# One pool of 1-MB places for all expert weights, up products split by w1 and w3, and half of the shared expert and the ranking behind the first up products

## The reference, cut to what matters

```python
scores = sigmoid(xf @ w_router)             # 64 experts, 8 groups, 4 groups and 8 experts chosen per token
w = w / sum(w) * 2.5                        # the weights of the 8 chosen experts
def expert_block(args):
    toks, e, wts = args
    return swiglu(xpad[toks], w1[e], w3[e], w2[e]) * wts[:, None]
def swiglu(x, w1, w3, w2):
    return (silu(x @ w1) * (x @ w3)) @ w2   # w1, w3: 1024 x 256; w2: 256 x 1024
y = routed + swiglu(xf, ws1, ws3, ws2)      # the shared expert takes all tokens
```

## Time and profile before

| | |
|---|---|
| median of 3 runs | 2468.27 us |
| the profiled execution | 2467.98 us, span 2466.4 us |
| PE busy | 2324.8 us, 94% of the span |
| DVE, ACT, POOL busy | 34%, 23%, 5% |
| DMA moved | 672.94 MB, mean 273 GB/s |
| chain that ended last | PE 82%, DMA 9%, DVE 4% |

### The profile page before, as it was taken

One profiled execution on the slowest core, in us unless ns is written; L12 is line 12 of the kernel. 1 busy time (PEld: TensorE's weight loads), 2 busy tenths in 40 slices (PEclk: granted clock), 3 DMA queues, 4 the chain that ended last, 5 costly groups with the idle time before them and its releaser, 6 DMA issues.

```text
span 2466.4 us, 30431 instructions
## 1 busy us (share of the span) xinstructions
PE 2324.8 (94%) x11979; PEld 1543.9 (63%) x11979; DVE 845.8 (34%) x2149; ACT 568.6 (23%) x1227; POOL 122.6 (5%) x179
## 2 busy tenths in 40 slices
PE   7998999999999898998999989898998999999998
PEld 4857887555455454767896545554546787754764
DVE  0477633212212111297623212121211644421264
ACT  2233412111111112123302111111112433321254
POOL 4020000000000000010000000000000000001110
PEclk9999999999999998999999999999998999999999
DMA  9783583999999996953684999999986254240400
GB/s 334 264 311 118 206 328 132 418 415 414 413 404 414 417 400 248 319 197 137 225 326 183 407 414 414 417 395 414 415 368 190 92 186 143 84 145 29 159 1 18
DMA packets 206890, 672.94 MB, mean 273 GB/s; under 512 B 14000, under 2 KB 74648, under 8 KB 156816
## 3 DMA queue, kind: packets, MB, share of 16 engines
q1 hardware_dynamic: 200064, 656.87, 68.9%
q0 software_dynamic: 6240, 13.99, 1.7%
q10 hardware_dynamic: 432, 0.01, 0.0%
HBM read 661.38 MB, written 9.45 MB: 272 GB/s over the span
## 4 chain that ended last, share of the span: by engine, by line
PE 82%; DMA 9%; DVE 4%; ACT 2%; issue 2%; SPq 0%; ACTq 0%; POOL 0%; DVEq 0%
PE ps L278 46%; PE ps L2182 11%; PE ps L2217 7%; DMA ring<-in_ab_w_in 4%; PE ps L2233 3%; PE ps L1762 2%; DMA ring<-in_w 2%; DMA cst<-in_ab_w_in 2%; PE ps L1210 1%; DVE ar L1349 1%; PE ps L2864 1%; PE ps L3477 1%; PE ps L698 1%; DMA ring<-in_w_mod 1%; DMA ar<-in_w 1%
## 5 line engine op out<-in xcount | busy, mean ns | idle before, releaser
L278 PE MATMUL ps<-hT,ring 128*128 128x256 f32 (+2 forms) x2352 | 546.0, 388 | 3.4 <-ACT ar L1578 1.9
L278 PEld LDWEIGHTS ps<-hT,ring 128*128 128x128 f32 (+1 forms) x2352 | 442.2, 191 | 101.4 <-issue 37.1
L2182 PE MATMUL ps<-ring,ar 128*32 128x512 f32 (+2 forms) x1056 | 291.9, 613 | 20.2 <-DMA ring<-in_w 14.1
L2182 PE MATMUL ps<-ar 128*64 128x512 f32 (+1 forms) x992 | 292.3, 614 | 9.1 <-DMA ar<-in_w 9.0
L2182 PEld LDWEIGHTS ps<-ring,ar 128*32 128x32 f32 (+2 forms) x1056 | 90.7, 128 | 174.9 <-issue 162.0
L2217 PE MATMUL ps<-ring,ar 128*32 128x512 f32 (+2 forms) x808 | 182.3, 596 | 5.4 <-DVE ar L2365 3.0
L2499 DVE SCALAR_TENSOR_TENSOR exact_parts<-ps,ar,exact_parts 128x512 fp32r<-128x512 f32 x100 | 75.1, 751 | 284.5 <-ACT exact_parts L2345 278.9
L278 PE MATMUL ps<-xT,ring 128*128 128x256 f32 x576 | 134.6, 394 | 15.0 <-DMA ring<-in_ab_w_in 14.0
L2475 DVE TENSOR_TENSOR ar<-ar,ps 128x256 f32<-128x256 f32 x50 | 21.1, 421 | 351.3 <-ACT ar L2332 351.3
L278 PE MATMUL ps<-ring,ar 128*128 128x512 f32 x320 | 139.8, 593 | 0.9 <-DVE ar L3706 0.9
L2182 PEld LDWEIGHTS ps<-ar 128*64 128x64 f32 (+1 forms) x992 | 82.5, 126 | 91.4 <-issue 87.2
(11 more groups left out here) (461 smaller groups left out, 2782.2 us busy)
## 6 DMA issues: line engine op xcount, KB each, us to landing
ring<-in_w SPq DMA_DIRECT2D x233, 1024.0 KB, 15.9
ar<-in_w SPq DMA_DIRECT2D x124, 1024.0 KB, 12.8
ring<-in_w_mod SPq DMA_DIRECT2D x36, 2048.0 KB, 11.9
ring<-in_w_in SPq DMA_DIRECT2D x28, 2048.0 KB, 11.7
ring<-in_ab_w_in SPq DMA_DIRECT2D x51, 1024.0 KB, 10.9
cst<-in_w SPq DMA_DIRECT2D x27, 1024.0 KB, 12.5
ring<-in_w_out SPq DMA_DIRECT2D x4, 2048.0 KB, 10.5
ring<-in_ab_w_out SPq DMA_DIRECT2D x2, 4096.0 KB, 13.0
```

Of the source, the lines that this page charges most:

```text
L278: ins = te.matmul(o, l, r, start=(first and i == 0), stop=(last and i == len(pairs) - 1), skip_group_check=lax)
L2182: ins = te.matmul(b[cols, :], K.x_b[:, kk, in_pair(p, cols)], weights_up(K, l, r)[:, :, kk, :], start=(kk == 0), stop=(kk == 7))
```

## The change

Every expert matrix is now a load of its own (keys w1, w3, w2) with a place of its own. All 16 places form one pool: four halves of the wide buffers, the consts place, and the 11 places of the ring. The loads stand in the order in which the passes need them: w1 of all experts of a pass, then w3, then the fill, then w2. A place is given to the next load by when it comes free in that order. For the places of the ring the table `RING_HELD` says, for each layer, what the mixer left there. `pe_up` does the w1 products of the pass in one bank, with 256 columns each, and then the w3 products in another; w1's places are released in between. ACT takes silu behind the w1 products and DVE multiplies behind the w3 products. `pe_moe_start` leaves the second half of the shared expert's down products and the ranking to `pe_experts`, which does them between the first up products and the first turn. The transposed lists have another place in SBUF, since silu now writes their old one before the ranking reads them. Where the next stage begins in the ring is no longer the position behind the last load but a pair of places that comes free early (`next`).

```diff
+NOTHING, THIRD, OUT, ROUTER, SHARED_UP, SHARED_DOWN = -12, -10, -8, -6, -4, 0.5
+RING_HELD = [{1: NOTHING, 2: THIRD, 3: THIRD, 4: OUT, 5: OUT, 6: OUT, 7: OUT, 8: ROUTER, 9: SHARED_UP, 10: SHARED_UP,
+              0: SHARED_DOWN},
+             {10: NOTHING, 8: THIRD, 9: THIRD, 0: OUT, 1: OUT, 2: OUT, 3: OUT, 4: ROUTER, 5: SHARED_UP, 6: SHARED_UP,
+              7: SHARED_DOWN}]
+def in_turn(l):
+    out = []
+    for p, of in enumerate(PASS):
+        out += [(p, p + 0.3, "w1", r) for r, _ in of]
+        out += [(p + 0.3, p + 0.45, "w3", r) for r, _ in of]
+        if p in FILL_AT[l]:
+            out.append((p + 0.5, p + 0.65, "fill", FILL_AT[l][p]))
+        out += [(p + 0.7, p + 1, "w2", r) for r, _ in of]
+    return out
 def places(l):
-    up = {("wide", 0): (-1, None), ("wide", 1): (-1, None), **{("slot", n): (-1, None) for n in range(3)}}
-    down = {("consts", 0): (-1, None), ("last", 0): (-1, None), **{("half", u): (-1, None) for u in range(4)}}
+    free = {("consts", 0): (NOTHING, None), **{("wide", n): (THIRD, None) for n in range(4)},
+            **{("ring", u): (held, None) for u, held in RING_HELD[l].items()}}
...
+    for start, end, name, r in in_turn(l):
+        if l == 1 and start >= CONSTS_PASS:
+            free.pop(("consts", 0), None)
+        place = min(free, key=lambda k: free[k][0])
+        assert free[place][0] < start
+        out[name, r] = place, free[place][1]
+        free[place] = end, (name, r)
...
+    out["next"] = min(range(UNITS - 1), key=lambda u: max(free["ring", u][0], free["ring", u + 1][0]))
...
+            pos = K.where[key[1]]["next"]
...
 def pe_moe_start(K, l):
...
-    for n in range(4):
-        i, q = divmod(n, 2)
...
-        if n == 1:
-            yield from pe_first_slots(K, l)
-            yield from pe_selected(K, l, 0)
-            yield from pe_lists_turned(K, l)
-    yield from pe_lists_ranked(K, l)
+    yield from pe_shared_down(K, l, 0)
+    yield from pe_first_slots(K, l)
+    yield from pe_selected(K, l, 0)
+    yield from pe_lists_turned(K, l)
 def pe_up(K, l, p):
     te = K.te
...
+    for name, read in (("w1", "silu"), ("w3", "g")):
+        b = yield from K.bank((read, l, p))
...
+        for kk in range(8):
+            for r, cols in PASS[p]:
+                ins = te.matmul(b[cols, 0:256], K.x_b[:, kk, in_pair(p, cols)], w[r][:, kk, :], start=(kk == 0),
+                                stop=(kk == 7))
+        ins.then_inc(*K.pe(name, l, p, ps=b))
+        for r, _ in PASS[p]:
+            K.pe.also("used", name, l, r)
 def pe_experts(K, l):
...
         yield from pe_up(K, l, p)
+        if p == 0:
+            yield from pe_lists_ranked(K, l)
+            yield from pe_shared_down(K, l, 1)
 def act_experts(K, l):
...
-        ac.wait_ge(*(yield ("up", l, p)))
+        ac.wait_ge(*(yield ("w1", l, p)))
 def dve_experts(K, l):
...
         ve.wait_ge(*(yield ("silu", l, p)))
+        ve.wait_ge(*(yield ("w3", l, p)))
```

More of the change, by code:

```diff
@@ L419, in shared @@
         K.plan(("down", l, EXPERTS), 1, [(lambda f: k_major(f, D, 2), I["ws2"][l].rearrange("(j p) n -> p j n", j=2))])
[L421 to L443, removed]
     def experts(l):
@@ L451, in experts @@
         kind, r = K.where[0]["consts"]
[L452 to L457, removed]
+        consts = [("used", kind, 0, r)] if l else [("ctx_turned", 3)]
+        for _, _, name, r in in_turn(l):
+            (kind, u), last = where[name, r]
+            if name == "fill":
                 n, g = FILL[r]
                 src = abw.rearrange("(p k) n -> p k n", k=8)[:, :, FILL_COL[n] * D + g * 256:FILL_COL[n] * D + g * 256 + 256]
-                parts = [(lambda f: k_major(f, 256), src)]
+                part = (lambda f: k_major(f, 256)), src
             else:
-                parts = [(lambda f: f[:, 0:UNIT], ("w2", 2))]
-            if kind in ("slot", "half", "last"):
+                part = (lambda f: f[:, 0:UNIT]), (name, 2 if name == "w2" else 8)
+            if kind == "ring":
                 place = kind, u
             else:
-                start = first[kind][u] if kind == "wide" else first[kind]
-                place = views(name, kind, u), [("used", before[0], l, before[1])] if before else start
-            K.plan((name, l, r), len(parts), parts, place)
+                place = K.cst_place if kind == "consts" else K.wbuf[u // 2][:, u % 2, :]
+                place = place, [("used", last[0], l, last[1])] if last else wide[u // 2] if kind == "wide" else consts
+            K.plan((name, l, r), 1, [part], place)
     def ctx_parts(key, first, n):
@@ L572, in sp_program @@
     for n, (key, under, parts) in enumerate(K.loads):
-        if key[0] in ("up", "down") and FIXED <= key[2] < EXPERTS and key[1:] not in expert:
+        if key[0] in ("w1", "w3", "w2") and key[2] >= FIXED and key[1:] not in expert:
             sp.wait_ge(*(yield ("ranked", key[1])))
@@ L2209, in pe_down @@
     for r, _ in PASS[p]:
-        te.wait_ge(*(yield ("ring", "down", l, r)))
+        te.wait_ge(*(yield ("ring", "w2", l, r)))
     for q in range(2):
```

74 lines of the change are left out of this document (26 added, 48 removed).

## The result

| | median of runs | range | profiled execution |
|---|---|---|---|
| before, run again beside the changed kernel | 2465.91 us (16 runs) | 2463.28 to 2469.69 | 2467.98 us |
| changed kernel | 2471.10 us (16 runs) | 2468.51 to 2473.35 | 2470.19 us |

The ratio is 1.0022, with a 95% interval of 1.0015 to 1.0029: the change makes the kernel 5.4 us slower, between 3.7 and 7.1. I had forecast 2467.5 us and "no change to be measured" as the likeliest verdict. The two profiled executions differ by only 2.2 us, since that of before lies 2.1 us above the median of its kernel and that of the changed kernel 0.9 under its own; so the traces are compared here by place, and sums go by the medians.

A forecast was written before the change was run, and what follows sets the result against it. Each MoE was taken to end by the stream of weight loads, though PE is busy 94%. Terms -9.4 + 10.7 + 0.8 = +2.1 us, taken as -0.5: 2467.5 us; own range 2463 to 2472.5, wider range 2456 to 2480.

The forecast's parts named there:

- Layer 0: First layer's MoE: 6.6 us less standstill of the load stream and 2.8 us gained at the end, -9.4 us.
- Layer 1: Second layer's MoE: table misfits the ring, standstill 52.2 us against 41.3; +10.9 - 0.2 = +10.7 us.
- the split: Up products in 256-column halves: 0.15 us more PE per pass, 0.8 us in all, most beside waits for loads.
- the ledger: Hand account of loads and PE steps in both kernels, 2.59 us per load; ends before's layers 1.0 and 3.1 us early.
- a second gap: Layer 1's load stream: 15.1 us more standstill, until the moved second half of the shared down products ends.
- Rival 1: Layer 1's late stream is paid back where PE is behind: 2460 us; chance 0.27.
- rival 2: Layer 0's gain doesn't arrive because loads wait for places in strict order: -3 and +10.7, 2476 us; chance 0.16.
- rival 4: Layer 1's wait on the router is harmless, -9 us in each layer: 2450 us; chance 0.06.
- Sum: Whole kernel: -9.4 + 10.7 + 0.8 = +2.1 us, then -0.5 taken between +2.1 and -1.3, giving 2467.5 us.
- rival 3: Up products: weight loads of column tiles show, 1.9 us per pass, about +10 and +15, 2493 us; chance 0.07.
- The moved steps: Ranking and half the shared down products behind pass 0's up products: same instructions, fill a wait, cost under 1 us.
- The end of a pass: Last pass of four: only down products (3.6 us) behind the last landing, 2.8 us gained in layer 0, little in layer 1.

The follow-up runs named there:

- e1_table: Changed kernel with layer 1's row of `RING_HELD` rewritten to what the ring really holds there: 2458.72 us, ratio 0.9975 to the kernel before.
- e3_unmoved: Changed kernel with the second half of the shared down products and the ranking back ahead of the first up products: 2463.87 us, ratio 0.9986 to before.
- e4_late0: Changed kernel with layer 0's row of `RING_HELD` spoiled the way layer 1's is wrong: 2483.67 us, ratio 1.0070 to the kernel before.
- e6_pad: Kernel before, with 0.44 us more of PE in each up product by issuing one step twice: 2478.44 us, ratio 1.0049.
- e5_both: Changed kernel with layer 1's table repaired and both moved steps back ahead of the first up products: 2457.29 us, ratio 0.9969 to before.
- e7_split4: Kernel before, with each up product in four sweeps of 128 columns instead of one of 512: 2484.22 us, ratio 1.0081.
- e8_move: Kernel before, with only the second half of the shared down products moved behind the first up products: 2484.80 us, ratio 1.0076.
- e2_split: Kernel before, with only the up products split into two sweeps of 256 columns: 2470.68 us, ratio 1.0018.

## Why the prediction was wrong

**What held.** Both terms of the order of loads, nearly in size. Layer 0: -9.4 us in the sum; the trace has -8.9 from the router on, or -7.2 if the router's slower products in before are left out. Layer 1: +10.7 in the sum, 11.1 in the trace. These differences of the traces also hold what the split costs, which the two terms leave out, so that they fit as closely as this is in part luck. By the experiments the ledger is somewhat high: 14.8 for each table, where 11.6 and 11.9 were measured. The named causes are the ones seen: no load into ar before 1297 us (1296.94), and a second gap that ends with the shared down products (1332.20 + 3.70; the next load leaves at 1335.9). The cause in layer 1 is shown by e1_table, that the move has a part in it by e3_unmoved, and the worth of layer 0's order by e4_late0. Rival 1 (the debt is swallowed), rival 2 (layer 0's gain doesn't arrive) and rival 4 (the router's wait is harmless) are thereby out.

**The step that failed** is the last one, in "The split" and "Sum": how much of PE's own time reaches the end. The prediction said that 0.15 us per pass, 7.5 us in all, costs 0.8, since most lies beside waits for loads; and it then took the sum of +2.1 down to -0.5, on the ground that a slower PE forgives a late stream. Measured, the split gives PE only some 2.6 us more and costs 4.4 [2.0, 6.7], and a plain addition of 21.5 us brings 12.1 (e6_pad), which is over half and not a tenth. Put together, with the split's measured term and no discount:

| kernel | layer 0 | layer 1 | split | sum | measured |
|---|---|---|---|---|---|
| changed kernel | -9.4 | +10.7 | +4.4 | +5.7 | +5.4 [3.7, 7.1] |
| e3_unmoved | -9.4 | +2.0 | +4.4 | -3.0 | -3.5 [-5.7, -1.2] |
| e1_table, e5_both | -9.4 | -4.1 | +4.4 | -9.1 | -6.2 [-9.1, -3.5], -7.6 [-10.6, -4.4] |

The terms of layer 1 are the ledger's for that order of loads. That the first two rows fit to 0.5 us (the third is 1.5 and 2.9 off) is luck, since the split's term alone has 2.4 us of uncertainty to either side, and the table takes it to be the same in every order of the loads, which no run tests. So the ledger was right to within some 3 us on what the order of loads is worth, and wrong on what PE's time is worth. Its two small errors against the trace of before (1.0 and 3.1 us early) may have been the hint: I used them to lower the sum by 2.6 us, and in my reading now they said that PE counts for more. Why the split costs more than e6_pad's share of its PE time stays open. The step rested on a DMA share of 1.01, which I read as a stream with no slack.

**Weight loads (rival 3).** Even sweeps of 128 columns take 7.18 us in a pass of four (e7_split4), and the up products of the changed kernel, w1 and w3 together, take 6.91 to 7.14 us where nothing is awaited. By the rule of the Trainium skill that the prediction weighed ("TensorE: Matmul & The Clock Gate", Part 3, on row and column tiling), every added weight load would show; the trace of e7_split4 disagrees again, as four times the loads add 0.17 us.

**The moved steps.** In the sum they were "under 1 us". As a statement on PE that held (e5_both against e1_table), but the release that moves with them is the larger thing, as e8_move shows with +18.7 us. The prediction had it in layer 1 (the second gap of 15.1 us), under the table; by e3_unmoved it is 8.9 us (7.2 by the medians), nearly all of it in layer 1, where its trace has 551.1 us from the router's products to the last scatter in place of 558.2.

**The end of a pass.** I gained 2.8 us in layer 0 by having only the down products (3.6 us) behind the last load. They do stand there alone, but a wait comes ahead of them, and they then take 5.13 us in place of 3.64 in layer 1, and in layer 0 go from 923.83 to 929.09. Beside the 6.6 us of the standstill, the trace's -7.2 to -8.9 in layer 0 leaves 0.6 to 2.3 of the 2.8, with the split's cost still in it.

## What to carry to other kernels

A DMA share of 1.01 doesn't say that the stream of loads is the bound: look also at the waits of the queue that issues them. Where it waits for the engine's releases most of the time, don't put added engine time at nothing: here 39 to 73% of it reached the end. When a step is moved, look first at what it releases and who waits for that in an in-order queue, and only then at where its instructions fall. And a table that repeats what another program part decides should be compared with that part's outcome: here eleven numbers were worth some 12 us.

## What the runs showed of the hardware that I had not expected

- Halving the columns of a matmul at the same total costs PE little: 7.01 to 7.09, 7.07 to 7.15 and 7.18 us for 64, 128 and 256 matmuls of a pass of four (before, e2_split, e7_split4). At 128 columns a pass of one, with full weight loads, shows more: 7.34 us in place of 7.06.
- With 18,123 matmuls in the program in place of 11,979, PE stops 11 times in the up products for 1.1 to 1.7 us with no wait to name, each time with a packet of the instruction queue that starts 2.4 to 2.6 us before the stop's end; with 14,027 matmuls (e2_split) it has no such stop.
- Executions of one kernel lie 10 us apart (before: 2461.95 to 2472.69 in 24 runs) and the longer ones show a lower mean clock (0.974 to 0.976 in four of the five longest, 0.980 and 0.979 in the two shortest). A single trace can't settle an effect of 5 us.
